# Moving the second layer's modulations from one feed-forward part beside another, and cutting that part in four groups

## Chip, cores and metric

The kernel runs on one core of one Trainium2 chip. The metric is the device time of one execution in microseconds, as the median of several executions. Times in the views of the profile come from one further execution, taken by the hardware profiler.

## What is computed

Two networks run one after the other on 512 tokens of width 1024, all in float32. The first is one layer of a hybrid block (16 meta tokens in front): a feed-forward part, a mix of forgetting attention and retention, and a second feed-forward part. The second network has two layers over 512 latent and (in the first layer) 256 context tokens. Cut to what matters here:

```
def swiglu(x, w_in, w_out):
    a, b = jnp.split(x @ w_in, 2, axis=-1)        # w_in 1024 x 2*2816
    return (jax.nn.silu(a) * b) @ w_out           # w_out 2816 x 1024

for l in range(2):
    mod   = split_cols(silu(c)     @ w_mod[l] + b_mod[l], (1024,) * 6)   # six vectors of 1024, for the latents
    mod_x = split_cols(silu(c_ctx) @ w_mod[l] + b_mod[l], (1024,) * 6)   # and six for the context
    h = layer_norm(x) * (1 + sc1) + sh1           # shift and scale come from mod
    ...                                           # mixing sublayer, gated by g1, layer norm
    x = layer_norm(ALPHA * x + g2 * swiglu_2(modulate(x, sh2, sc2), w_ffn_in[l], w_ffn_out[l])) ...
```

`w_mod[l]` is 1024 x 6144, so each layer's modulations read 25 MB and give only 12 vectors.

## The kernel before

**Layout.** Activations stand feature by feature: a tile is 128 features by a chunk of tokens. Each float32 operand is split into a high and a low part in fp32r, and each product is three matmuls into the same PSUM bank: high x high, high x low, low x high (`mm3`, lines 1334 to 1336; they show in the profile as weight tile and moving tile, each h or l).

**Weights.** SyncE loads every weight tile (128 x 1024, 512 KB, or less for output weights) in one written order into a ring of four buffers `Wf`. ScalarE copies it to a high part (L2054) and VectorE subtracts to get the low part (L2758); both go into a slot, three slots "base" and three "top" in the parts of interest. How many entries of the order the two engines may convert ahead of the one in use is `look`, set by the steps `("ahead", n)`; `AHEAD` is 1. TensorE waits for the low part at the first chunk of a tile (`tile_item`).

**Feed-forward parts.** 22 pairs of 128 inner features. For pair j the items "fa" (gate half, 8 slices of 3 matmuls) and "fb" (value half) give the hidden slice j: ScalarE takes the silu out of PSUM (L2332), VectorE multiplies (L3114), ScalarE makes the high part (L2342), POOL the low part (L3685). After a group of pairs, eight items "fo" multiply the hidden slices of the group with the output weights, and VectorE adds each result to `H` (`residual`, L3126). The groups are 8, 7 and 7 pairs in "f1" and "f2" (both parts of the first network) and in "g0" (first latent layer), and 5, 5, 6, 6 in "g1". f1 has chunks of 256 and 272 tokens, f2 two of 256, g0 three of 256 (context first). In f2 the second chunk runs four tiles behind the first. In g0 a `Group` deals out the items: the chunk that is furthest behind and whose norm is done is next, at most five tiles apart. The last group's "fo" items of g0 go chunk by chunk, and load their weights anew for each chunk, 24 weights for 24 items.

**Modulations.** A step `("mod", l, m)` takes one raw tile of `w_mod` from the ring; VectorE multiplies it with the silu of each of the two conditioning vectors and sums (`modulation`, L2972 and L2974, both 128 x 1024). Before the first step "vectors" lets POOL load the two vectors, spread over all partitions, into `CR` (L3701), and "rows" lets ScalarE take their silu (L2193). The 48 steps of layer 0 lie beside f1, those of layer 1 beside f2. Layer 1's results are first used after g0.

**Order.** All engines run the same written sequence. The planner `woven` writes it with a clock of its own: each matmul item costs 0.345 us for each slice, and the steps of a norm's chain (`chain`: mean, centre, square, root, second, both) are put in where their due times fall; later items wait for a gate, such as "chunk 0 of the next norm is done". After g0's last group come the norm of each chunk (d0 joined with a1) and the next layer's projections (`projection_items`), whose first eight items need chunk 0 alone, three need chunk 1, then three chunk 2. `FILL` puts filling matmuls (L1322) at a few places: 13 in the last chunk's mean, 15 and 3 ahead of the last chunk's first projection.

Of the kernel before, what the change touches and what calls it, by code (L numbers as in the profile page):

```python
# [4 lines left out]
F32 = mybir.dt.float32  # L5
# [12 lines left out]
T1 = NMETA + TX  # L18
NFF = 22
CH = [(0, 8), (8, 7), (15, 7)]  # L20
CHS = {"f1": CH, "f2": CH, "g0": CH, "g1": [(0, 5), (5, 5), (10, 6), (16, 6)]}
PLAIN_PAIRS = 3
UNITS_AHEAD = 7
ALPHA = (2 * 2) ** 0.25
# [101 lines left out]
class Shared:  # L126
# [42 lines left out]
    def buffers(self):  # L169
# [36 lines left out]
        self.H2[0], p = at("H2h", [128, 8, TX], F32R, P1)  # L206
        self.H2[1], p = at("H2l", [128, 8, TX], F32R, p)
        self.TM2, p = at("TM2", [128, 2, 256], F32, p)
        CR2, CR2e = at("CR2", [128, 1024], F32, p)

        self.YT, p = at("YT", [128, 4, 1024], F32, P1)
        self.YB, P2 = at("YB", [128, 8, TX], F32, p)
# [45 lines left out]
        self.OT, _ = at("OT", [128, 6, 1024], F32, P0)  # L258
        self.O[0], p = at("OH", [128, 8, 768], F32R, P4)
        self.O[1], P5 = at("OL", [128, 8, 768], F32R, p)  # L260
        self.H3[0], p = at("H3h", [128, 8, 768], F32R, P4)
        self.H3[1], p = at("H3l", [128, 8, 768], F32R, p)
        self.X2[1], P6 = at("X2l", [128, 8, 768], F32R, P5)
        self.XC2, _ = at("XC2", [128, 8, 768], F32, P5)
        assert CR2e <= P5
        self.PA, p = at("PA", [128, 3, 272], F32, P6)
        self.TM3, pm = at("TM3", [128, 3, 264], F32, p)
        self.MS, pm = at("MS", [128, 2, 128], F32, pm)
        self.WM_at = pm
        self.WM, pm = at("WM", [128, 2, 8, 64], F32, pm)  # L270
        assert pm <= TOP
        CR3, p = at("CR3", [128, 1024], F32, p)
        self.JK, p = at("JK", [128, 1024], F32, p)
        assert p <= TOP
        self.CR = [(CR1[:, 0, :], CR1[:, 1, :]), (CR2[:, :], CR3[:, :])]
        self.weight_slots("top", 3, TOP)

        self.QC, p = at("QC", [128, 3, 768], F32, P4)
# [538 lines left out]
class Group:  # L817

    def __init__(self, tiles, chunks, lead, gate):
        self.tiles, self.chunks, self.lead, self.gate = tiles, chunks, lead, gate
        self.at = {c: 0 for c in chunks}

    def due(self, ready):
        low = min(self.at.values())
        for c in sorted(self.chunks, key=lambda c: (self.at[c], c)):
            i = self.at[c]
            if i < len(self.tiles) and i - low < self.lead and ready(self.gate(c)):
                self.at[c] += 1  # L830
                k, x, nk = self.tiles[i]
                return (*k, x, c), 0.345 * nk, None
        return None

    def done(self):
        return min(self.at.values()) == len(self.tiles)


def woven(items, chains):
# [96 lines left out]
def second_sequence(p):  # L936

    f, n3, a = p.ffns["f2"], p.norms["n3"], p.norms["a0"]
    items = [(("open", "mixed", [(p.mm, ("branch", 1, 7, 0))]), 0, None)]
    items += [(("wo", m, c), 2.8, None) for m, c in lagged(range(8), 2, 4)]  # L940
    ends = [last_of(items, "wo", c, None) for c in (0, 1)]
    items[8:8] = [(("ahead", 2), 0, None)]
    items += [(("close", "mixed"), 0, None), (("open", "top", [(p.mm, ("mixout", 7, 1))]), 0, None)]
    items.append((("vectors", 1), 0, None))
    tiles = ffn_items(f, 4, lambda c: c, mod_steps(1))
    items += tiles[:8] + [(("ahead", AHEAD), 0, None)] + tiles[8:]
    done = last_of(items, "fb", 1, f)
    ends += [last_of(items, "fo", c, f) for c in (0, 1)]
    items += [(("close", "top"), 0, None), (("open", "latent", [(p.mm, ("fo", "f2", 2, 7, 1))]), 0, None)]
    items += projection_items(0, lambda c: 2 + c)  # L950
    chains = [(chain([n3], c), ends[c], 1.9) for c in (0, 1)] + [(chain([a], 0), done, 0.0)]
    chains += [(chain([a], c + 1), ends[2 + c], (3.5, 13.0)[c]) for c in (0, 1)]
    return woven(items, chains)
# [39 lines left out]
def latent_sequence(p, l):  # L993

    f, b, c_, d = p.ffns[f"g{l}"], p.norms[f"b{l}"], p.norms[f"c{l}"], p.norms[f"d{l}"]
    nc = len(f.chunks)
    ci = 1 if l == 0 else 0
    order = [3, 4, 5, 6, 7, 0, 1, 2]
    items = [("open", "top", p.fence(f"att{l}"))] + [("of", l, ci, k) for k in (3, 4)] + [("groups", l)]
    items += [("of", l, ci, k) for k in (5, 6, 7)] + [("scales", l)]  # L1000
    items += [("early", l, m, 0) for m in (0, 1)] + [("of", l, ci, k) for k in order[5:]] + [("ahead", 3)]
    for m in range(8):
        items.append(("oo", l, m, 0))
        if l == 0:
            items.append(("of", l, 0, order[m]))
        if m in (2, 5):
            items.append(("moments", b, m == 5))
    items = [(x, 2.8 if x[0] == "oo" else 0.5, None) for x in items]
    items += [(("oo", l, m, c), 2.8, None) for c in range(1, nc) for m in range(8)]
    if l == 0:  # L1010
        items[-2:-2] = [(("moments", d, False), 0, None)]
        items.append((("moments", d, True), 0, None))
    tiles = []
    last = len(CHS[f.tag]) - 1
    for n, (j0, nj) in enumerate(CHS[f.tag]):
        for j in range(j0, j0 + nj):
            tiles += [(("fa", f), j, 8), (("fb", f), j, 8)]
        if n < last:
            tiles += [(("fo", f), (n, m), nj) for m in range(8)]
    if l == 0:  # L1020
        items.append(Group(tiles, range(nc), 5, lambda c: c))
    else:
        items += fast_items(f, tiles)
    items += [(("fo", f, (last, m), c), 0.345 * CHS[f.tag][last][1], None) for c in range(nc) for m in range(8)]
    items += [(("ahead", AHEAD), 0, None), (("close", "top"), 0, None)]
    chains = [(chain([b], c), ("oo", l, 7, c), 3.0 if c == 2 else 2.0) for c in range(nc)]
    ends = [("fo", f, (last, 7), c) for c in range(nc)]
    if l == 0:
        items.append((("open", "latent", [(p.mm, ("fo", "g0", 2, 7, 2))]), 0, None))
        items += projection_items(1, lambda c: 3 + c)  # L1030
        chains += [(chain([d], c), ends[c], 2.0) for c in range(nc)]
        return woven(items, chains)
    chains += [(chain([d], c), ends[c], 2.0) for c in range(nc)]
    chains.append(([(("combine", f, x), 0.0, 2.5) for x in range(6)], ("fa", f, 0, 1), 0.5))
    return woven(items, chains)
# [1711 lines left out]
class VectorE(Engine):  # L2747
# [214 lines left out]
    def modulation(self, l, m):  # L2962

        p, e = self.p, self.e
        u = self.get("wmod", (l, m), 1024, True)
        w = p.Wf[:, u % NW, :]
        e.wait_ge(*p.w_arrived(u))
        if m == 0:
            e.wait_ge(*p.act.of(("rows", l, 1)))
        if m or l:  # L2970
            e.wait_ge(*p.dve.of(("first", l, m - 1) if m else ("first", l - 1, 47)))
        e.scalar_tensor_tensor(p.JK[:, :], w, 1.0, p.CR[l][0], ALU.mult, ALU.mult, p.MOD[:, l, m, 0:1]).then_inc(  # L2972
            *p.dve.did(("first", l, m)))
        e.scalar_tensor_tensor(w, w, 1.0, p.CR[l][1], ALU.mult, ALU.mult, p.MOD[:, l, m, 1:2]).then_inc(  # L2974
            *p.dve.did(("w", u), ("sum", l, m)))
        self.finished(u)
        if m % 8 < 7:
            return
        x = p.MOD[:, l, m - 7:m + 1, :]
        b0 = VEC[f"bmod{l}"][0] + m - 7  # L2980
        b = p.V[:, b0:b0 + 8].unsqueeze(2).broadcast_to([128, 8, 2])
        e.wait_ge(*p.dve.of(("sum", l, m)))
        if m // 8 in (2, 5):
            e.tensor_tensor(x, x, b, ALU.add).then_inc(*p.dve.did(("biased", l, m)))
            e.wait_ge(*p.dve.of(("biased", l, m)))
            e.tensor_scalar(x, x, 1.0 / ALPHA, None, ALU.mult).then_inc(*p.dve.did(("mod", l, m)))
        else:
            e.scalar_tensor_tensor(x, x, 1.0 if m // 8 in (1, 4) else 0.0, b, ALU.add, ALU.add).then_inc(
                *p.dve.did(("mod", l, m)))
# [653 lines left out]
class PoolE(Engine):  # L3643
# [8 lines left out]
    def step(self, what, *a):  # L3652
        p, e = self.p, self.e
        if what == "fb":
            self.hidden_low(*a)
        elif what == "load_sums":
            self.load_sums(*a)
        elif what == "apply":
            self.lows(*a)
        elif what == "both":  # L3660
            N, i, g = a
            if g == 1:
                self.lows(N.then, i)
        elif what == "bar":
            self.bar(*a)
            if a[0] == "mix":
                self.fence("mix")
                e.dma_start(p.CS[:, :, :], p.A["rope1"]).then_inc(*p.load(("rope1",)).did("in"))
                e.wait_ge(*p.load(("rope1",)).of("in"))
            else:  # L3670
                self.latent_loads(int(a[0][1]))
        elif what == "vectors":
            e.wait_ge(*p.mm.of(("mixout", 7, 1)))
            self.vectors(*a)
        elif what == "rturn":
            self.ret_turn(*a)
        elif what == "tick":
            self.tick(*a)
# [479 lines left out]
```

## Time and profile before

| | us |
|---|---|
| median of 3 executions | 3278.16 |
| lowest, highest | 3277.17, 3283.82 |
| the profiled execution | 3296.36 |
| its span in the trace | 3294.5 |
| TensorE busy | 3177.3 (96%) |
| VectorE busy | 1801.6 (55%) |
| ScalarE busy | 1391.9 (42%) |
| mean granted TensorE clock | 0.993 of full |

Times in the rows below are from the start of the span. A busy TensorE can still be slowed, since the ends of matmuls are modelled; only the distance of their starts and the waits tell the rest.

### The profile page before, as it was taken

The page shows a single profiled execution, that of the slowest core. Times are in us where ns is not written, and L with a number is a line of the kernel's source. Part 1 is how long each engine was busy: PE and PEld are TensorE (multiplying, and loading weights), DVE is VectorE, ACT ScalarE, POOL GpSimd, SP SyncE. Part 2 cuts the span into 40 slices and gives each one's busy share as a digit, 9 for nine tenths or more (in the row PEclk, how much of TensorE's full clock was granted, in tenths as well). Part 3 has the DMA queues.
Part 4 walks back from the last instruction along what each step waited for, and adds up shares of the span by engine and source line. Part 5 has one row for each costly group of instructions (what it writes and reads, how often), then busy time and mean ns, then how long its engine had stood idle before and what let it go on. Part 6 is the DMA issues. An engine that isn't in the chain of part 4 may idle for free. (4 is left out here: it accounts for less than half of the span.)

```text
span 3294.5 us, 60366 instructions
## 1 busy us (share of the span) xinstructions
PE 3177.3 (96%) x24458; PEld 2954.1 (90%) x24458; DVE 1801.6 (55%) x3099; ACT 1391.9 (42%) x2533; POOL 481.9 (15%) x471
## 2 busy tenths in 40 slices
PE   7999999999999999999999999999999999989998
PEld 7999988797778899998889889999998889979997
DVE  4666643536644456666435774222226646777766
ACT  4222232336633332225447755212124647665545
POOL 1010110036500010110103301101010103211110
PEclk9999999999999999999999999999999999999999
DMA  4445422122222334443211341211213311426663
GB/s 150 178 162 178 154 71 78 58 75 61 57 74 93 106 129 169 173 177 128 68 37 27 118 127 48 65 59 58 71 59 121 100 64 33 139 71 166 161 154 106
DMA packets 107075, 339.68 MB, mean 103 GB/s; under 512 B 12145, under 2 KB 16497, under 8 KB 106673
## 3 DMA queue, kind: packets, MB, share of 16 engines
q1 hardware_dynamic: 97616, 311.65, 28.9%
q0 software_dynamic: 8752, 23.65, 3.3%
q8 instruction: 198, 3.24, 0.4%
q14 instruction: 77, 0.62, 0.1%
q10 hardware_dynamic: 432, 0.52, 0.0%
HBM read 324.38 MB, written 2.10 MB: 99 GB/s over the span
## 5 line engine op out<-in xcount | busy, mean ns | idle before, releaser
L2758 DVE TENSOR_TENSOR r_Wbasel<-r_Wf,r_Wbaseh 128x1024 fp32r<-128x1024 f32 (+3 forms) x286 | 358.7, 1255 | 509.5 <-ACT r_Wbaseh L2054 509.0
L2054 ACT ACTIVATE r_Wbaseh<-r_Wf 128x1024 fp32r<-128x1024 f32 (+3 forms) x286 | 291.2, 1022 | 419.1 <-PE PS L1336 316.2
L2758 DVE TENSOR_TENSOR r_Wtopl<-r_Wf,r_Wtoph 128x1024 fp32r<-128x1024 f32 (+3 forms) x147 | 174.0, 1185 | 207.5 <-ACT r_Wtoph L2054 207.0
L1334 PE MATMUL PS<-r_X2h,r_Wbaseh 128*128 128x256 f32 (+1 forms) x888 | 276.7, 312 | 5.5 <-POOL r_X2l L3717 2.5
L1335 PE MATMUL PS<-r_X2l,r_Wbaseh 128*128 128x256 f32 (+1 forms) x888 | 269.0, 303 | 0.0
L1336 PE MATMUL PS<-r_X2h,r_Wbasel 128*128 128x256 f32 (+1 forms) x888 | 269.0, 303 | 0.0
L2054 ACT ACTIVATE r_Wtoph<-r_Wf 128x1024 fp32r<-128x1024 f32 (+3 forms) x147 | 145.9, 1001 | 141.6 <-PE PS L1336 54.6
L1334 PE MATMUL PS<-r_X1h,r_Wbaseh 128*128 128x512 f32 (+2 forms) x480 | 180.7, 376 | 8.5 <-ACT r_K L2455 3.2
L1334 PEld LDWEIGHTS PS<-r_X2h,r_Wbaseh 128*128 128x128 f32 x888 | 166.8, 188 | 19.0 <-POOL r_X2l L3717 3.3
L1336 PEld LDWEIGHTS PS<-r_X2h,r_Wbasel 128*128 128x128 f32 x888 | 169.1, 190 | 8.0
L1335 PEld LDWEIGHTS PS<-r_X2l,r_Wbaseh 128*128 128x128 f32 x888 | 166.8, 188 | 10.2 <-issue 2.6
L2332 ACT ACTIVATE r_TM<-PS 128x256 f32<-128x256 f32 (+1 forms) x160 | 61.4, 385 | 253.4 <-PE PS L1336 249.9
L1335 PE MATMUL PS<-r_X1l,r_Wbaseh 128*128 128x512 f32 (+2 forms) x480 | 168.3, 351 | 0.0
L1336 PE MATMUL PS<-r_X1h,r_Wbasel 128*128 128x512 f32 (+2 forms) x480 | 168.0, 350 | 0.0
L3114 DVE TENSOR_TENSOR r_TM<-r_TM,PS 128x256 f32<-128x256 f32 (+1 forms) x160 | 67.1, 420 | 148.7 <-PE PS L1336 136.5
L1334 PE MATMUL PS<-r_X2h,r_Wtoph 128*128 128x256 f32 x504 | 141.7, 281 | 0.0
L1335 PE MATMUL PS<-r_X2l,r_Wtoph 128*128 128x256 f32 x504 | 141.5, 281 | 0.0
L1336 PE MATMUL PS<-r_X2h,r_Wtopl 128*128 128x256 f32 x504 | 141.5, 281 | 0.0
L2974 DVE SCALAR_TENSOR_TENSOR r_Wf<-r_Wf,r_CR 128x1024 f32<-128x1024 f32 x96 | 131.1, 1366 | 0.0
L3378 DVE TENSOR_REDUCE r_SM<-PS 128x1 f32<-128x768 f32 (+6 forms) x184 | 120.9, 657 | 18.2 <-PE PS L1878 12.5
L3126 DVE SCALAR_TENSOR_TENSOR r_H<-PS,r_MOD,r_H 128x256 f32<-128x256 f32 x136 | 65.4, 482 | 118.4 <-PE PS L1336 117.8
L2972 DVE SCALAR_TENSOR_TENSOR r_JK<-r_Wf,r_CR 128x1024 f32<-128x1024 f32 x96 | 117.5, 1224 | 0.0
(544 smaller groups left out, 11105.8 us busy)
## 6 DMA issues: line engine op xcount, KB each, us to landing
r_Wf<-in_wmod SPq DMA_DIRECT2D x96, 512.0 KB, 3.6
r_Wf<-in_f_in SPq DMA_DIRECT2D x88, 512.0 KB, 4.4
r_Wf<-in_g_in SPq DMA_DIRECT2D x69, 512.0 KB, 3.5
r_Wf<-in_w_o SPq DMA_DIRECT2D x40, 512.0 KB, 4.4
r_Wf<-in_f_out SPq DMA_DIRECT2D x32, 448.0 KB, 4.2
r_Wf<-in_g_out SPq DMA_DIRECT2D x32, 448.0 KB, 3.4
r_SR<-in_g_in SPq DMA_DIRECT2D x38, 256.0 KB, 3.7
r_SR<-in_g_in POOLq DMA_DIRECT2D x38, 256.0 KB, 5.4
```

Of the source, the lines that this page charges most:

```text
L1334: self.e.matmul(o, wh, xh, start=first, stop=False)
L1335: self.e.matmul(o, wh, xl, start=False, stop=False)
L1336: return self.e.matmul(o, wl, xh, start=False, stop=last)
L2054: e.activation(p.w(i, cols)[0], p.Wf[:, i % NW, 0:cols], ACT.Copy).then_inc(*p.hi.did(i))
L2332: e.activation(f.tm(j, c), p.psb(p.bank(("fa", f.tag, j, c)), f.chunks[c][1]), ACT.Silu).then_inc(*p.act.did(("silu", f.tag, j, c)))
L2758: e.tensor_tensor(l, p.Wf[:, i % NW, 0:cols], h.bitcast(F32), ALU.subtract).then_inc(*p.lo.did(i))
L2972: e.scalar_tensor_tensor(p.JK[:, :], w, 1.0, p.CR[l][0], ALU.mult, ALU.mult, p.MOD[:, l, m, 0:1]).then_inc(*p.dve.did(("first", l, m)))
L2974: e.scalar_tensor_tensor(w, w, 1.0, p.CR[l][1], ALU.mult, ALU.mult, p.MOD[:, l, m, 1:2]).then_inc(*p.dve.did(("w", u), ("sum", l, m)))
L3114: e.tensor_tensor(x, x, p.psb(p.bank(("fb", f.tag, j, c)), f.chunks[c][1]), ALU.mult).then_inc(*p.dve.did(("gated", f.tag, j, c)))
L3126: e.scalar_tensor_tensor(hk, p.psb(p.bank(("fo", f.tag, ci, m, c)), n), f.gate(m, c0), hk, ALU.mult, ALU.add).then_inc(*p.dve.did(("res", ...
L3378: e.tensor_reduce(p.SM[:, u % 4:u % 4 + 1], p.psb2(b, 0, d.n), AX, ALU.max, negate=True).then_inc(*p.dve.did(("max", A.id, u)))
```

## The change

The 48 modulation steps of layer 1, with "vectors" and "rows", leave f2 and are handed to g0's `Group` as `others`: after 12 tile items, one of the 51 entries is dealt out after every 180/51 = 3.5 tile items (of 204 in the group; the last group's 24 "fo" items come after it). The first of the entries is `("ahead", AHEAD)`, so `look` goes from 3 to 1 there. g0's groups become 6, 6, 5, 5 pairs, so that `H3` needs six slices; in the space of the other two lie the conditioning vectors `CR2` and a scratch tile `JK2` of layer 1. "vectors" now waits for the last output projection before g0.

```diff
-CHS = {"f1": CH, "f2": CH, "g0": CH, "g1": [(0, 5), (5, 5), (10, 6), (16, 6)]}
+CHS = {"f1": CH, "f2": CH, "g0": [(0, 6), (6, 6), (12, 5), (17, 5)], "g1": [(0, 5), (5, 5), (10, 6), (16, 6)]}
...
-        CR2, CR2e = at("CR2", [128, 1024], F32, p)
...
-        self.H3[0], p = at("H3h", [128, 8, 768], F32R, P4)
-        self.H3[1], p = at("H3l", [128, 8, 768], F32R, p)
+        self.H3[0], p = at("H3h", [128, 6, 768], F32R, P4)
+        self.H3[1], p = at("H3l", [128, 6, 768], F32R, p)
+        CR2, p = at("CR2", [128, 2, 1024], F32, p)
+        JK2, p = at("JK2", [128, 1024], F32, p)
+        assert p <= P5
...
-        CR3, p = at("CR3", [128, 1024], F32, p)
-        self.JK, p = at("JK", [128, 1024], F32, p)
+        JK1, p = at("JK1", [128, 1024], F32, p)
         assert p <= TOP
-        self.CR = [(CR1[:, 0, :], CR1[:, 1, :]), (CR2[:, :], CR3[:, :])]
+        self.CR, self.JK = [(t[:, 0, :], t[:, 1, :]) for t in (CR1, CR2)], (JK1, JK2)
...
-    def __init__(self, tiles, chunks, lead, gate):
+    def __init__(self, tiles, chunks, lead, gate, others=()):
         self.tiles, self.chunks, self.lead, self.gate = tiles, chunks, lead, gate
-        self.at = {c: 0 for c in chunks}
+        self.at, self.others, self.said = {c: 0 for c in chunks}, others, 0

     def due(self, ready):
-        low = min(self.at.values())
+        low, n = min(self.at.values()), len(self.others)
+        if self.said < n and self.said * (len(self.at) * len(self.tiles) - 24) < (sum(self.at.values()) - 12) * n:
+            self.said += 1
+            return self.others[self.said - 1], 0, None
...
-    items.append((("vectors", 1), 0, None))
-    tiles = ffn_items(f, 4, lambda c: c, mod_steps(1))
+    tiles = ffn_items(f, 4, lambda c: c)
...
-        items.append(Group(tiles, range(nc), 5, lambda c: c))
+        items.append(Group(tiles, range(nc), 5, lambda c: c, [("ahead", AHEAD), ("vectors", 1)] + mod_steps(1)))
...
-        items.append((("open", "latent", [(p.mm, ("fo", "g0", 2, 7, 2))]), 0, None))
+        items.append((("open", "latent", [(p.mm, ("fo", "g0", 3, 7, 2)), (p.dve, ("sum", 1, 47))]), 0, None))
...
-            e.wait_ge(*p.mm.of(("mixout", 7, 1)))
+            e.wait_ge(*p.mm.of(("oo", 0, 7, 2)))
```

## Rows read from the trace of the kernel before

**Rows 1.** The page: busy engines, and the commonest conversion groups.

```profile
span 3294.5 us, 60366 instructions
PE 3177.3 (96%) x24458; PEld 2954.1 (90%) x24458; DVE 1801.6 (55%) x3099; ACT 1391.9 (42%) x2533; POOL 481.9 (15%) x471
...
L2758 DVE TENSOR_TENSOR r_Wbasel<-r_Wf,r_Wbaseh 128x1024 fp32r<-128x1024 f32 (+3 forms) x286 | 358.7, 1255 | 509.5 <-ACT r_Wbaseh L2054 509.0
L2054 ACT ACTIVATE r_Wbaseh<-r_Wf 128x1024 fp32r<-128x1024 f32 (+3 forms) x286 | 291.2, 1022 | 419.1 <-PE PS L1336 316.2
```

**Rows 2.** Windows: length; PE, PEld, DVE, ACT, POOL; clock, DMA share, GB/s.

```profile
1163.00:1535.00 372.00, 363.41 (x3132) 356.47 (x3133) 240.44 (x367) 115.77 (x176) 42.81 (x45) 1.00 0.45 156
2018.00:2504.00 486.00, 486.00 (x4128) 485.93 (x4126) 128.69 (x185) 111.33 (x187) 45.88 (x62) 1.00 0.22 69
```

**Rows 3.** Waits of TensorE, 1163 to 1533: us in total, times, longest.

```profile
PE PS L1334 <- DVE r_Wbasel L2758: 3.1, 6, 0.7
PE PS L1334 <- DVE r_Wtopl L2758: 3.1, 5, 1.1
```

**Rows 4.** Windows of 10 us; the first count is of matmuls.

```profile
1240.00:1250.00 10.00, 10.00 (x90) 10.00 (x89) 8.03 (x13) 2.78 (x4) 1.21 (x1) 1.00 0.50 167
1290.00:1300.00 10.00, 10.00 (x87) 10.00 (x86) 6.94 (x11) 2.92 (x4) 0.73 (x1) 1.00 0.49 177
2260.00:2270.00 10.00, 10.00 (x87) 10.00 (x87) 2.09 (x4) 2.17 (x4) 1.48 (x2) 1.00 0.14 46
```

**Rows 5.** Timeline of TensorE: starts of matmuls.

```profile
2557.01 0.28 PE L1334 MATMUL PS<-r_H3h,r_Wtoph 128*128 128x256 f32 x1
...
2557.69 0.28 PE L1334 MATMUL PS<-r_X2h,r_Wbaseh 128*128 128x256 f32 x1
...
2010.96 0.39 PE L1334 MATMUL PS<-r_X2h,r_Wbaseh 128*128 128x256 f32 x1 [1.24 <-POOL r_X2l L3717]
...
2011.42 0.28 PE L1334 MATMUL PS<-r_X2h,r_Wbaseh 128*128 128x256 f32 x1
...
2012.48 0.28 PE L1334 MATMUL PS<-r_X2h,r_Wbaseh 128*128 128x256 f32 x1
```

**Rows 6.** VectorE groups: 1163 to 1533 (two), 2018 to 2503.

```profile
L2974 DVE SCALAR_TENSOR_TENSOR r_Wf<-r_Wf,r_CR 128x1024 f32<-128x1024 f32 x48 | 65.5, 1364 | 0.0
L2972 DVE SCALAR_TENSOR_TENSOR r_JK<-r_Wf,r_CR 128x1024 f32<-128x1024 f32 x48 | 59.1, 1231 | 0.0
L3126 DVE SCALAR_TENSOR_TENSOR r_H<-PS,r_MOD,r_H 128x256 f32<-128x256 f32 x56 | 27.1, 484 | 90.2 <-PE PS L1336 90.2
```

**Rows 7.** DMA issues over the span: KB each, median us to landing.

```profile
r_Wf<-in_wmod SPq DMA_DIRECT2D x96, 512.0 KB, 3.6
r_CR<-in_c POOLq DMA_DIRECT2D x4, 512.0 KB, 5.3
```

**Rows 8.** Timeline of VectorE and POOL at g0's end.

```profile
2508.20 2.35 DVE L3007 TENSOR_TENSOR r_H<-r_H,PS 128x1024 f32<-128x1024 f32 x2
2519.83 0.43 DVE L3047 TENSOR_SCALAR r_RS<-PS 128x256 f32<-128x256 f32 x1 [1.74 <-ACT r_RS L2267]
...
2524.65 0.41 DVE L3063 TENSOR_TENSOR r_SQ<-PS,r_RS 128x256 f32<-128x256 f32 x1
...
2553.73 2.41 POOL L3717 TENSOR_TENSOR r_X2l<-r_XC,r_X2h 128x1024 fp32r<-128x1024 f32 x1 [70.06 <-ACT r_X2h L2306]
...
2613.63 2.36 POOL L3717 TENSOR_TENSOR r_X2l<-r_XC,r_X2h 128x1024 fp32r<-128x1024 f32 x1 [19.59 <-ACT r_X2h L2306]
```

**Rows 9.** Waits of TensorE, 2503 to 2620.

```profile
PE PS L1625 <- ACT r_SQ L2251: 4.4, 2, 2.3
```

**Rows 10.** A window and two starts of TensorE in the last layer.

```profile
2930.00:2940.00 10.00, 6.88 (x40) 6.60 (x41) 5.10 (x4) 6.17 (x10) 3.10 (x2) 0.83 0.05 10
...
2935.20 0.41 PE L1334 MATMUL PS<-r_X3h,r_Wtoph 128*128 128x256 f32 x1
2935.42 0.41 PE L1335 MATMUL PS<-r_X3la,r_Wtoph 128*128 128x256 f32 x1
```

More of the change, by code:

```diff
@@ L260, in buffers @@
         self.O[1], P5 = at("OL", [128, 8, 768], F32R, p)
-        self.H3[0], p = at("H3h", [128, 8, 768], F32R, P4)
-        self.H3[1], p = at("H3l", [128, 8, 768], F32R, p)
+        self.H3[0], p = at("H3h", [128, 6, 768], F32R, P4)
[3 more added lines that the diff above has]
+        assert p <= P5
         self.X2[1], P6 = at("X2l", [128, 8, 768], F32R, P5)
         self.XC2, _ = at("XC2", [128, 8, 768], F32, P5)
-        assert CR2e <= P5
         self.PA, p = at("PA", [128, 3, 272], F32, P6)
@@ L835, in done @@
     def done(self):
-        return min(self.at.values()) == len(self.tiles)
+        return min(self.at.values()) == len(self.tiles) and self.said == len(self.others)
 def woven(items, chains):
@@ L2971, in modulation @@
             e.wait_ge(*p.dve.of(("first", l, m - 1) if m else ("first", l - 1, 47)))
-        e.scalar_tensor_tensor(p.JK[:, :], w, 1.0, p.CR[l][0], ALU.mult, ALU.mult, p.MOD[:, l, m, 0:1]).then_inc(
+        e.scalar_tensor_tensor(p.JK[l][:, :], w, 1.0, p.CR[l][0], ALU.mult, ALU.mult, p.MOD[:, l, m, 0:1]).then_inc(
             *p.dve.did(("first", l, m)))
```

## The prediction

> **What bounds the kernel now.** I read the page first. TensorE is busy 96% of the span, VectorE 55%, so work taken off VectorE is worth nothing by itself; only what it makes TensorE wait for counts [rows 1]. Then the windows, stage by stage [rows 2]. In the first net's second feed-forward part ("f2", 1163 to 1535 us) VectorE is at 240/372 = 65% and the DMA engines move 156 GB/s. In the steady part of the first latent layer's feed-forward part ("g0", 2018 to 2504) TensorE is busy all 486 us, VectorE 26%, DMA 69 GB/s. So the 48 modulation steps leave a full stage for an empty one, but TensorE is nearly full in both: the whole prize is the waits in f2 and what happens at g0's two ends.
>
> The waits say how much there is: in f2 TensorE waited 3.1 + 3.1 = 6.2 us, eleven times, for a weight's low half (L2758), which VectorE had not finished [rows 3]. In g0's steady part the view of waits is empty (no idle time in rows 2 either).
>
> A second thing shows only in windows of 10 us. Without idle time TensorE starts 90 matmuls of 256 columns in some and 87 in others [rows 4]. Between starts there are 113.3 ns in the fast pace (2557.01 to 2557.69 is six) and 117.8 ns in the slow one (2010.96 aside, 2011.42 to 2012.48 is nine) [rows 5]; the granted clock is 1.00, its level of 2.4 GHz, in both. Going through the starts, the pace changes only where TensorE restarts after a gap, and then holds. In f2 it is slow from 1262 to 1307, from 1395 to 1440 and for some 10 us later, 100 us in all; in g0 it is slow from the restart at 2010.96 until 2504 without a break. Slow costs 4.5/117.8 = 3.8%.
>
> **The change, part by part.**
>
> *Modulations out of f2.* 48 pairs of VectorE instructions of 1.23 and 1.36 us, 125 us, leave [rows 6], with 48 loads of 512 KB [rows 7]. VectorE falls to 115/372 = 31%, near g0's 26%, where TensorE never waits, and the ring of four load buffers serves weights alone. I take all 6.2 us. Without restarts the pace in which f2's body begins should hold; it is fast there before the first step's work (the last restart at 1165 was a fast one), so the 100 us of slow pace go too: 3.8 us. Bounds of that: if f2 ran slow throughout, 264 us more would be slow (1170 to 1534 less the 100), each 113.3 growing by 4.5: +10.4 us; if the share of slow pace stays, 0.
>
> The Trainium skill ("TensorE: Matmul & The Clock Gate", section "Back-to-back issue gap") gives one gap for warm matmuls, N/2.4 + 2.5 ns, which is 109 ns at 256 columns. The rows differ from it and have two paces; by that rule no pace term would exist and the sum would hold the 6.2 us alone.
>
> *Modulations into g0.* The 51 added entries (a lookahead setting, "vectors", "rows", 48 steps) are spread over 204 - 24 tile items, one in 3.5 items, which is 3.5 x 24 x 0.118 = 10 us; each costs VectorE 2.6 us. VectorE: 129 + 125 + 12 (below) = 266 of 486 us, 55%. DMA: 25 MB more over 486 us, 69 + 52 = 121 GB/s against the 156 that f2 lived with [rows 2]. More telling than shares is the lead. In f2 a weight serves two chunks, and the second runs four tiles behind, so five of six slots are held and a new weight has 5.4 us. In g0 three chunks go in step, a weight serves 3 items of 2.8 us = 8.5 us; in the output groups 6.4 us (six slices) and 5.3 us (five). The work that can stand before the low half is one step 2.6, a gating or residual 0.48 and the conversions 1.0 + 1.25 [rows 1]: 5.3 us. It fits, with nothing to spare at five slices. The new lookahead of 1 (g0 ran at 3) still lets the next weight through across one step. I take 0; the bounds are 0 and f2's rate of 0.13 us a step, 6.2 us. SyncE's queue holds a step's load between two weights: 3.6 us to landing [rows 7], four ring slots are some 18 us ahead. POOL issues two loads of 512 KB (5.3 us to landing) four items, 11 us, before ScalarE needs them; if they were late ScalarE would stand still, but eight PSUM banks hold 22 us of TensorE's work. The scratch tiles lie in slices 6 and 7 of H3, which six-slice groups don't touch, and the O tiles there are dead by then.
>
> *Four groups.* The matmuls are the same: 22 slices x 8 x 3 chunks x 3. VectorE gets 24 more residual adds of 0.484 us, 11.6 us [rows 6], hidden under TensorE. The third boundary needs the last pair's hidden half; two boundaries of the same kind cost nothing today, and a step of 2.6 us before them still ends within the 7.4 us that the item order leaves. 0, at worst 1 us.
>
> *g0's end.* Here I expect a loss. The last group goes chunk by chunk, 24 items with a weight each. They shrink from 21 matmuls (2.4 us) to 15 (1.75 us), and run now at lookahead 1 instead of 3: a weight is converted two items ahead, 3.5 us, not four, 9.8 us. Yet the norm chain of a finished chunk puts blocks on VectorE: the root 2519.83 to 2525.06, 5.2 us; the centring 2.35; the second root and its products [rows 8]. Today three conversions run ahead of the root and TensorE loses nothing to weights there (its largest waits, 4.4 us in all, are for the chain itself) [rows 9].
>
> Stepping the queues from the end of chunk 0 (today 2501.7), with these durations: waits for weights of about 1.7 us after the centring, 2.3 after the first root, 2.1 and 2.2 around the second root's products; all 16 items of the other chunks end after 46 us (today 2557.7 - 2501.7 = 56). But the written order, made with 1.725 us an item, now has chunk 1's root ahead of chunk 0's last products, so chunk 0's inputs for the next projections are done after about 60 us (root at 42.7 + 1.6, ScalarE free at 48, root 5.2 to 54, products 2.5 and 3.1, high and low halves) against 54.4 today (POOL's low half 2553.73 + 2.41) [rows 8]. From there the projections need 44.6 us until the last chunk's second half (8 + 3 items of 2.75, the chain's 3.5, 18 filling matmuls 7.9, half an item). The total work is the same and 16 x 6 = 96 matmuls fewer lie behind chunk 0, so it ends 96 x 0.116 = 11.1 us later than today. New mark: 2501.7 + 11.1 + 60 + 44.6 = 2617.4; today 2616.0 [rows 8]. +1.3 us. Bounds: chunk 0 ready at 53 (the chain unimpeded), -5.7; at 68, +9.3.
>
> **Sum.** -6.2 - 3.8 + 0 + 0 + 1.3 = -8.7 us. The profiled execution took 3296.4 us (span 3294.5 and 1.9 around it), 18.2 above the median of 3278.2; the sum is a difference and I set it against the median: 3269.5 us. That 18.2 us are also what a fast g0 would be worth warns me that timed runs may sit in other paces.
>
> **Rivals.**
> - *g0 flips to the fast pace.* One restart in g0, from a step that makes a weight late, or another phase at its start. 486 x 3.8% = 18.6 us for all of it. For it: most restarts in f2 went fast. Against: few waits are expected there. 3269.5 - 18.6 = 3251; half of it 3260.
> - *f2 settles in the slow pace.* Nothing restarts it any more. -6.2 + 1.3 + 6.7 (170 us more slow than today) to + 10.4: 3280 to 3284. Against: its last restart before the steps was a fast one, and that part of the order stays.
> - *No pace effect.* The share of slow pace stays what it is, in f2 and in g0: -6.2 + 1.3, 3273. For it: whatever picks the pace is not known, and f1, whose chunks are 256 and 272 wide, is slow nearly throughout. The single gap on the Trainium skill's page ("TensorE: Matmul & The Clock Gate") would give this too.
> - *The steps are late in g0* (slower). VectorE's 2.6 us before a low half, at lookahead 1, in the output groups of 5.3 us a tile. It decides from 0.2 us a step: 48 x 0.2 = 9.6 eats the gain; at 0.5, +24, 3294. For it: f2 did so at 4.8 us a tile (42 matmuls). Against: the lead above.
> - *The end costs more.* Chunk 0 ready after 68 us: +9.3. An idle stretch there can also lower the clock: after 3.79 us idle at 2933 the granted clock reads 0.83 over 10 us and starts are 210 to 220 ns apart, the 1.2 GHz level, for 4 us, 2 us lost [rows 10]. 3278 to 3280.
>
> **Chances.** Forecast 0.40 (own range 3262 to 3276); fast g0 0.20; slow f2 0.12; no pace effect 0.13; late steps 0.10; dear end 0.05. Range 3251 to 3284, which leaves out the better half of fast g0 and most of late steps. What a measurement of this kernel can tell from no change is about 0.2%, 6.6 us. Faster by more: 0.27 + 0.18 + 0.06 + 0.02 = 0.53. Slower by more: 0.10 + 0.03 + 0.02 = 0.15. Within: 0.32.
>
> **What would show it.** Right: no wait of an L1334 on L2758 in f2, and 90 matmuls in its 10 us windows; g0's steady part still without waits; in the last group new waits on L2758 of 1 to 2 us, and an idle stretch of TensorE before the first projection. Wrong: waits on L2758 through g0's body, or 90 in its windows instead of 87; f2's windows at 87; a last group without waits for weights.

## The result, and the profile after

The kernel after takes 3298.20 us (median of 4, 3296.84 to 3299.51), the kernel before 3278.59 on the same chip: ratio 1.0056, 95% interval 1.0044 to 1.0069. It is slower by 0.56%, 18 to 20 us. I had forecast 3269.5.

In the kernel after, the lines I follow stand two further down: L1334 to L1336 are L1336 to L1338, L2758 is L2760, L2239 is L2241. First the same windows as [rows 2], then one over the tail of g0 and one of 10 us in it.

```profile
1163.00:1535.00 372.00, 369.85 (x3262) 365.42 (x3262) 135.99 (x178) 122.55 (x191) 37.27 (x46) 1.00 0.30 94
2018.00:2504.00 486.00, 484.51 (x4287) 481.57 (x4286) 262.24 (x432) 121.16 (x207) 47.35 (x58) 1.00 0.36 121
2480.00:2620.00 140.00, 100.35 (x761) 89.77 (x760) 83.50 (x112) 69.88 (x118) 9.27 (x7) 0.88 0.30 95
2590.00:2600.00 10.00, 5.49 (x25) 5.50 (x26) 8.08 (x9) 5.78 (x6) 2.35 (x1) 0.50 0.38 121
```

In the 372 us of f2 TensorE now starts 3262 matmuls and not 3132: 130 more, at 113.3 ns 14.7 us. VectorE is at 136/372 = 37% there, and its 262 us in g0 cost TensorE nothing before the last group. The loss is in the third row: 40 us of 140 idle. Before, the same 140 us had TensorE busy for 130.31:

```profile
2480.00:2620.00 140.00, 130.31 (x1066) 118.76 (x1066) 98.69 (x128) 80.46 (x128) 10.61 (x9) 0.98 0.35 110
```

The waits of TensorE from 2455 to 2640 in the kernel after: total, times, longest.

```profile
PE PS L1336 <- DVE r_Wbasel L2760: 17.0, 4, 12.1
PE PS L1695 <- ACT r_PA L2241: 8.2, 1, 8.2
PE PS L1649 <- ACT r_PA L2241: 6.8, 1, 6.8
PE PS L1627 <- DVE r_H L3128: 4.7, 1, 4.7
PE PS L1336 <- DVE r_Wtopl L2760: 3.0, 2, 1.5
PE PS L1978 <- ACT r_SQA L2644: 0.3, 1, 0.3
```

40.0 us, where the first profile of before has 10.0 in this stretch. Four waits are long (12.1, 8.2, 6.8, 4.7), and all four begin after the last output item of g0 has ended (2524.8).

What stood in front of the weight for which TensorE waited 12.06 us shows in ScalarE's timeline, with TensorE's restart behind it:

```profile
2575.74 1.04 ACT L2056 ACTIVATE r_Wbaseh<-r_Wf 128x1024 fp32r<-128x1024 f32 x1
...
2576.95 2.06 ACT L2294 ACTIVATE r_H<-r_H,r_V 128x256 f32<-128x256 f32 x4
...
2580.82 2.08 ACT L2294 ACTIVATE r_H<-r_H,r_V 128x256 f32<-128x256 f32 x4 [0.96 <-DVE r_H L3069]
2584.72 2.08 ACT L2305 ACTIVATE r_XC<-r_XC,r_MOD 128x256 f32<-128x256 f32 x4 [1.82 <-DVE r_XC L3088]
2586.83 1.06 ACT L2308 ACTIVATE r_X2h<-r_XC 128x1024 fp32r<-128x1024 f32 x1
2587.79 2.06 ACT L2305 ACTIVATE r_XC<-r_XC,r_MOD 128x256 f32<-128x256 f32 x4
2589.88 1.06 ACT L2308 ACTIVATE r_X2h<-r_XC 128x1024 fp32r<-128x1024 f32 x1
2590.84 1.04 ACT L2056 ACTIVATE r_Wbaseh<-r_Wf 128x1024 fp32r<-128x1024 f32 x1
```
```profile
2594.51 0.58 PE L1336 MATMUL PS<-r_X2h,r_Wbaseh 128*128 128x256 f32 x1 [12.06 <-DVE r_Wbasel L2760]
2594.89 0.41 PE L1337 MATMUL PS<-r_X2l,r_Wbaseh 128*128 128x256 f32 x1
2595.10 0.41 PE L1338 MATMUL PS<-r_X2h,r_Wbasel 128*128 128x256 f32 x1
```

Between two conversions of weights (2575.74 and 2590.84) stand the second root, its products and both halves of chunk 2's last step. Chunk 2 is needed by TensorE last of all; the conversion behind its blocks is needed now. When TensorE restarts, its starts are 0.21 us apart: over the idle stretch the granted clock fell to the level of 1.2 GHz (0.50 in the window of 2590). Some 29 matmuls start at that distance, and they take about 3 us more than at the fast pace.

The cause is to be read in the written order. Items of TensorE are in brackets, a number behind "d0" is a chunk; both lists begin behind the last output item of g0.

```
before: second d0 1 [qk 6] mean d0 2 [qk 8] both d0 1 0, centre d0 2 [qk 9] [vc 0] square d0 2, both d0 1 1
        [vc 1] root d0 2 [vc 2] second d0 2, both d0 2 0, both d0 2 1 [vc 3] [qk 2, chunk 0] ...
after:  mean d0 2, centre d0 2, second d0 1 [qk 6] both d0 1 0, square d0 2 [qk 8] root d0 2,
        both d0 1 1 [qk 9] second d0 2, both d0 2 0, both d0 2 1 [vc 0] [vc 1] [vc 2] [vc 3] [qk 2, chunk 0] ...
```

Before, chunk 2's chain is spread over five items, from behind [qk 6] to ahead of [vc 3]; after, all of it stands ahead of [vc 0], over three items. TensorE reaches [vc 3] with weights that were converted ahead of the bunch's end; the wait of 12.06 us is for the weight of the item behind it, [qk 2, chunk 0]. The planner's clock ran with items of five slices; on it the chains of chunks 1 and 2 fell due while it waited for chunk 0, and it wrote them down there.

The other half of the surprise is the kernel before itself. Its first profiled execution took 3296.4 us, 18 more than its timed ones. So the first run is that kernel once more.

### The profile page after: what moved, and what is told of

It reads as the page before. It is cut to its first block and busy times, and to the rows that moved or that the text cites. A ratio compares the mean times of both kernels' runs of the same rounds, so it can differ in the third digit from the quotient of the medians.

```text
span 3295.0 us, 60461 instructions
## 1 busy us (share of the span) xinstructions
PE 3151.4 (96%) x24458; PEld 2933.8 (89%) x24458; DVE 1809.8 (55%) x3131; ACT 1388.7 (42%) x2541; POOL 480.1 (15%) x471
## 5 line engine op out<-in xcount | busy, mean ns | idle before, releaser
L2760 DVE TENSOR_TENSOR r_Wbasel<-r_Wf,r_Wbaseh 128x1024 fp32r<-128x1024 f32 (+3 forms) x291 | 359.4, 1237 | 565.6 <-ACT r_Wbaseh L2056 565.2
L1336 PE MATMUL PS<-r_X2h,r_Wbaseh 128*128 128x256 f32 (+1 forms) x864 | 271.0, 314 | 17.8 <-DVE r_Wbasel L2760 15.6
L2760 DVE TENSOR_TENSOR r_Wtopl<-r_Wf,r_Wtoph 128x1024 fp32r<-128x1024 f32 (+3 forms) x150 | 171.8, 1146 | 171.6 <-ACT r_Wtoph L2056 171.6
L1337 PE MATMUL PS<-r_X2l,r_Wbaseh 128*128 128x256 f32 (+1 forms) x864 | 262.3, 304 | 0.0
L1338 PE MATMUL PS<-r_X2h,r_Wbasel 128*128 128x256 f32 (+1 forms) x864 | 262.2, 303 | 0.0
L1336 PEld LDWEIGHTS PS<-r_X2h,r_Wbaseh 128*128 128x128 f32 x864 | 164.9, 191 | 31.1 <-DVE r_Wbasel L2760 17.2
L1336 PE MATMUL PS<-r_X1h,r_Wbaseh 128*128 128x512 f32 (+2 forms) x480 | 180.7, 377 | 8.6 <-ACT r_K L2457 3.2
L1337 PEld LDWEIGHTS PS<-r_X2l,r_Wbaseh 128*128 128x128 f32 x864 | 165.0, 191 | 10.4 <-issue 2.6
L1338 PEld LDWEIGHTS PS<-r_X2h,r_Wbasel 128*128 128x128 f32 x864 | 164.8, 191 | 8.0
L1338 PE MATMUL PS<-r_X1h,r_Wbasel 128*128 128x512 f32 (+2 forms) x480 | 168.0, 350 | 0.0
L1336 PE MATMUL PS<-r_X2h,r_Wtoph 128*128 128x256 f32 x528 | 146.0, 277 | 0.0
L1338 PE MATMUL PS<-r_X2h,r_Wtopl 128*128 128x256 f32 x528 | 145.8, 276 | 0.0
L3380 DVE TENSOR_REDUCE r_SM<-PS 128x1 f32<-128x768 f32 (+6 forms) x184 | 121.0, 657 | 17.1 <-PE PS L1880 11.0
L3687 POOL TENSOR_TENSOR r_H3l<-r_TM,r_H3h 128x256 fp32r<-128x256 f32 x66 | 54.8, 832 | 445.8 <-ACT r_H3h L2344 445.8
```

The costliest lines, as they stand in the source:

```text
L1336: self.e.matmul(o, wh, xh, start=first, stop=False)
L1337: self.e.matmul(o, wh, xl, start=False, stop=False)
L1338: return self.e.matmul(o, wl, xh, start=False, stop=last)
L2760: e.tensor_tensor(l, p.Wf[:, i % NW, 0:cols], h.bitcast(F32), ALU.subtract).then_inc(*p.lo.did(i))
L3380: e.tensor_reduce(p.SM[:, u % 4:u % 4 + 1], p.psb2(b, 0, d.n), AX, ALU.max, negate=True).then_inc(*p.dve.did(("max", A.id, u)))
```

## Experiments

Each was timed against the kernel before on the same chip, with as many runs as stand beside it (the first with one). Where two traces are compared I use the time between two marks in g0: the restart on chunk 2's second half at its start, and the same of the last chunk's first projection at its end.

**1. The kernel before once more.** No edit.

> The kernel before, once more with a profile, to see which of two things its first profiled execution of 3296.4 us (18 over its timed runs) was. Theory A (the pace of g0 differs from execution to execution, and the first profile caught a slow one): if this profile is near 3278, g0's windows of 10 us show 90 matmuls and not 87 and the stretch 2010 to 2504 is up to 18 us shorter. Rival B (profiling adds the 18 us everywhere): 3296 again, windows as before.

3280.78 us, and its windows:

```profile
2018.00:2504.00 486.00, 486.00 (x4298) 483.97 (x4297) 139.88 (x201) 121.96 (x202) 45.74 (x62) 1.00 0.23 74
2260.00:2270.00 10.00, 10.00 (x91) 10.00 (x90) 1.51 (x2) 3.26 (x6) 0.73 (x1) 1.00 0.16 48
```
```profile
2011.41 0.39 PE L1334 MATMUL PS<-r_X2h,r_Wbaseh 128*128 128x256 f32 x1 [1.28 <-POOL r_X2l L3717]
...
2598.03 0.38 PE L1334 MATMUL PS<-r_X2h,r_Wbaseh 128*128 128x256 f32 x1 [1.31 <-POOL r_X2l L3717]
```

4298 matmuls in the stretch where [rows 2] has 4128, 91 in the window where [rows 4] has 87. Between the marks (2598.03 - 2011.41) lie 586.6 us; in the first profile it is 2616.04 - 2010.96 = 605.1; the start is in [rows 5], and the end mark reads

```profile
2616.04 0.38 PE L1334 MATMUL PS<-r_X2h,r_Wbaseh 128*128 128x256 f32 x1 [1.29 <-POOL r_X2l L3717]
```

Theory A holds: the same program ran g0 in the slow pace once and in the fast pace here, and the difference of 18.5 us is that of the executions (3296.4 to 3280.8, 15.6) with 3 us elsewhere the other way. The timed median goes with the fast one. All twelve profiles of this section and that of the kernel after show g0 fast; the first one of before was the odd one of fourteen. The baseline for the marks is 586.6; in the kernel after they are at 1995.69 and 2617.67, 622.0 apart: 35.4 us lost, of which 40.0 - 10.1 = 29.9 are waits.

Where they are lost shows when the stretch is cut at two more starts: the first output item of chunk 1 (chunk 0's last one has then ended) and the first projection item. For the kernel after, with the end mark:

```profile
2478.60 0.28 PE L1336 MATMUL PS<-r_H3h,r_Wtoph 128*128 128x256 f32 x1
...
2544.44 0.78 PE L1336 MATMUL PS<-r_X2h,r_Wbaseh 128*128 128x256 f32 x1
...
2617.67 0.47 PE L1336 MATMUL PS<-r_X2h,r_Wbaseh 128*128 128x256 f32 x1
```

| us | start mark to end of chunk 0's output items | to the first projection | to the end mark |
|---|---|---|---|
| before, first profile | 490.5 | 56.2 | 58.4 |
| before, this run | 472.0 | 57.3 | 57.3 |
| after | 482.9 | 65.8 | 73.2 |

The first column grows by 10.9 us, because 96 more matmuls now lie ahead of that point. The other two grow by 8.5 and 15.9 us.

**2. The four groups alone.**

```diff
-CHS = {"f1": CH, "f2": CH, "g0": CH, ...
+CHS = {"f1": CH, "f2": CH, "g0": [(0, 6), (6, 6), (12, 5), (17, 5)], ...
```

> The kernel before with g0's groups 6, 6, 5, 5 alone: modulations stay in f2, lookahead stays 3, memory as before. Theory O (the order written for shorter last items puts all of chunk 2's norm chain ahead of the fourth projection item, and TensorE runs out of work twice): slower than before by 15 to 25 us, 3293 to 3304, with waits of TensorE of about 30 us between 2480 and 2620 and one of 10 us or more before the item vc 0. Rival L (it is the lookahead of 1 that the moved steps bring): within 3 us of before, 3276 to 3282.

3312.29 us (4 runs; before 3281.58), ratio 1.0096 (1.0082 to 1.0110): +30.7. Its waits in the tail:

```profile
PE PS L1334 <- DVE r_Wbasel L2758: 13.8, 2, 12.1
PE PS L1693 <- ACT r_PA L2239: 11.2, 2, 7.6
PE PS L1647 <- ACT r_PA L2239: 7.2, 1, 7.2
PE PS L1625 <- DVE r_H L3126: 3.3, 1, 3.3
```

The whole loss, and more, is in the groups, with the modulations still in f2 and the lookahead at 3. Theory O had the size of the waits (35.8 us with a small one of 0.3, the longest 12.1), but not the place of the longest, which stands ahead of [qk 2, chunk 0] and not of vc 0; and the time is 8 us above its range.

**3. The lookahead of 3 in the last group.** On the kernel after:

```diff
+    if l == 0:
+        items.append((("ahead", 3), 0, None))
     items += [(("fo", f, (last, m), c), 0.345 * CHS[f.tag][last][1], None) for c in range(nc) for m in range(8)]
```

> The kernel after, with the lookahead put back to 3 ahead of the last group's output items; its written order stays. Theory O (the order): the waits of 1.4 to 1.9 us for weights in the last group go, at most 6 us, but the long ones at 2525 to 2594 stay, since they lie where the lookahead is 3 in both kernels: 3292 to 3298. Rival L (the lookahead): most of the 30 us of waits go, 3268 to 3275.

3298.30 us (5 runs; before 3281.58), ratio 1.0054 (1.0041 to 1.0067): +16.7, where the kernel after has +19.6, and 0.3 above theory O's range. Between the marks are 616.6 us, 5.4 less than in the kernel after. The small waits of the last group are gone, and the others, 34.2 us, are those of run 2 but for one (10.4 where that has 12.1):

```profile
PE PS L1338 <- DVE r_Wbasel L2762: 12.2, 2, 10.4
PE PS L1697 <- ACT r_PA L2243: 11.2, 2, 7.6
PE PS L1651 <- ACT r_PA L2243: 7.2, 1, 7.2
```

The long waits stand where they stood, behind the last output item, where the lookahead is 3 in both kernels. The lookahead isn't the cause of the large part.

**4. The old order, on the kernel after.** The planner prices the last group's items at seven slices; items and instructions stay. The written tail is then that of before.

```diff
-    items += [(("fo", f, (last, m), c), 0.345 * CHS[f.tag][last][1], None) for ...
+    items += [(("fo", f, (last, m), c), 0.345 * (7 if l == 0 else CHS[f.tag][last][1]), None) for ...
```

> The kernel after, with the planner's price for the last group's output items put back to that of seven slices, which writes the tail in the same order as in the kernel before (chunk 2's steps spread between the projection items); nothing else changes. Theory O (the order): 3265 to 3278, 20 to 30 us faster than after, the wait of 12.06 us gone. Rival S (the items are simply too short to cover the chains, whatever the order): within 5 us of after, 3293 to 3299. Rival L (the lookahead of 1): the same as rival S.

3281.23 us (11 runs, 3270.62 to 3300.31; before 3281.58), ratio 1.0004 (0.9988 to 1.0019): 17 us less than the kernel after, 20.0 by what each has against its own runs of before, and 3 us above theory O's range. The runs spread over 30 us, so the second figure is not exact to more than a few us. The wait of 12 us is gone; what is left are three of about 3 us for weights in the last group:

```profile
PE PS L1336 <- DVE r_Wbasel L2760: 5.9, 2, 3.2
PE PS L1336 <- DVE r_Wtopl L2760: 3.1, 1, 3.1
```

**5. The new order, on the kernel before.** The opposite edit: groups of 8, 7, 7 with their seven-slice items, priced at five. Nothing else differs from the kernel before.

> The kernel before (8, 7, 7 pairs, modulations in f2, lookahead 3) with one thing changed: the planner prices the last group's output items at five slices, so that the tail of g0 is written in the order of the kernel after, while the items keep their seven slices. Theory O (the written order is what costs): slower than before by 15 to 30 us, 3297 to 3312, with waits of TensorE near 30 us in the tail and one of about 12 us for a weight ahead of vc 0. Rival S (short items leave the chains uncovered, the order alone is harmless): within 5 us of before, 3277 to 3287.

3302.57 us (5 runs; before 3279.12), ratio 1.0078 (1.0066 to 1.0090): +23.5.

```profile
PE PS L1334 <- DVE r_Wbasel L2758: 13.5, 2, 12.0
PE PS L1693 <- ACT r_PA L2239: 8.2, 2, 7.3
PE PS L1625 <- DVE r_H L3126: 6.0, 1, 6.0
PE PS L1647 <- ACT r_PA L2239: 4.9, 1, 4.9
```

The four long waits come with the order alone, long items or short. Of the 26.2 us between the marks (612.8 for 586.6), 12.9 lie ahead of the first projection and 13.3 behind it.

**6. Only chunk 2's chain later.** On the kernel after; the order of chunks 0 and 1 in the last group stays new.

```diff
-        chains += [(chain([d], c), ends[c], 2.0) for c in range(nc)]
+        chains += [(chain([d], c), ends[c], 12.0 if c == 2 else 2.0) for c in range(nc)]
```

> The kernel after, with only chunk 2's norm chain due 10 us later in the planner: its six entries then stand between the projection items again, while the order of the chains of chunks 0 and 1 in the last group stays that of after. Theory O2 (the loss is chunk 2's bunch in front of vc 0 alone): 3275 to 3283. Theory O1 (the late order of chunk 0's and 1's steps costs its share, the waits of 4.7, 6.8 and 8.2 us): 3285 to 3293. Rival S: 3294 to 3299.

3278.97 us (11 runs, 3272.74 to 3280.83; before 3279.12), ratio 0.9998 (0.9989 to 1.0007). Between the marks 601.1 us, 20.9 less than in the kernel after. By the times it takes away as much as the whole old order did in run 4 (which still has 9.0 us of waits for weights in the last group). Of the 20.9 us, 16.0 lie behind the first projection, which needs 57.2 us to the end mark, as in the kernel before: that part was chunk 2's bunch. Ahead of the first projection 61.0 us are left of 65.8, and there stands one long wait. It is for chunk 0's inputs: it ends with the first projection item, which needs chunk 0 alone, before chunk 2's chain has begun.

```profile
2538.14 0.55 PE L1336 MATMUL PS<-r_X2h,r_Wbaseh 128*128 128x256 f32 x1 [14.65 <-DVE r_X2l L3092]
```
```profile
PE PS L1336 <- DVE r_X2l L3092: 14.7, 1, 14.7
PE PS L1336 <- DVE r_Wbasel L2760: 3.5, 2, 1.9
PE PS L1336 <- DVE r_Wtopl L2760: 3.0, 2, 1.5
```

**7. The old order and the lookahead of 3.** The edits of 3 and 4 together.

> The kernel after with the old tail order and the lookahead of 3 in the last group, both. Theory: with the old order the lookahead matters (it left waits of 3.15, 3.17 and 2.74 us for weights and a stretch at 1.2 GHz behind them, 12 us in all against the second profile of before), so this takes 8 to 12 us off the run with the old order alone: 3269 to 3273. Rival (the order leaves no room for the lookahead, as it changed nothing with the new order): 3279 to 3283.

3268.88 us (7 runs, 3266.34 to 3276.12; before 3279.12), ratio 0.9975 (0.9965 to 0.9986): -10.2 against before, where run 4 has -0.35. With the old order the lookahead counts for 9.9 us (6.0 between the marks).

```profile
PE PS L1629 <- ACT r_SQ L2255: 4.4, 2, 2.3
PE PS L1651 <- ACT r_PA L2243: 4.0, 2, 2.2
PE PS L1629 <- DVE r_H L3130: 1.9, 1, 1.9
PE PS L1629 <- DVE r_H L3011: 1.6, 1, 1.6
PE PS L1338 <- DVE r_Wbasel L2762: 1.4, 1, 1.4
PE PS L1338 <- POOL r_X2l L3721: 1.3, 1, 1.3
```

The waits are 14.9 us with the small one. The marks are 2587.03 - 1995.33 = 591.7 us apart, 5.1 more than before. The first projection starts at 2528.24, 50.0 us behind chunk 0's output items, and from there 58.8 us pass to the end mark.

**8. A longer last group: 5, 5, 6, 6.** On run 7:

```diff
-"g0": [(0, 6), (6, 6), (12, 5), (17, 5)]
+"g0": [(0, 5), (5, 5), (10, 6), (16, 6)]
```

> As the run with both, but with g0's groups 5, 5, 6, 6 instead of 6, 6, 5, 5, so that the last group's 24 items have 18 matmuls each, not 15. Theory S (a part of the tail's cost is that short items cover less of the chains): 2 to 6 us below the run with both. Rival (the tail is bound by the chains' own length from the last output item on, which grows by nothing): within 1.5 us of it.

3272.90 us (12 runs, 3265.31 to 3282.37; before 3279.12), ratio 0.9981 (0.9971 to 0.9991). It is 4 us above run 7, where theory S had it 2 to 6 below and its rival within 1.5; the two intervals overlap, and between the marks it has 589.9 us, 1.8 less, so which is better stays open. The waits in its tail are 2.2 us less in all (12.7 for 14.9).

**9. A lookahead of 5 for the projections.** On the kernel after, in its own order:

```diff
-    items = [(("ahead", 3), 0, None)] + [(("qk", l, s, True, True, 0), 2.8, gate(0)) for s in (6, 8, 9)]
+    items = [(("ahead", 5 if l else 3), 0, None)] + ...
```

> The kernel after, in its own written order, with the lookahead in the second layer's projections at 5 instead of 3. Theory Q (the wait of 12.06 us is a conversion queued behind chunk 2's blocks on ScalarE and VectorE: lookahead 3 reaches from the step before the bunch to vc 3 and no further, the next weight stands behind): two more weights pass ahead of the bunch, the wait shrinks to about half and 5 to 10 us come back, 3288 to 3293. Rival (that weight is late for another reason, its load or its slot): 3296 to 3300.

3299.00 us (6 runs, 3293.77 to 3303.54; before 3282.17), ratio 1.0050 (1.0038 to 1.0063). The profile goes with theory Q: TensorE takes nine items, not seven, before the wait, which is now for the weight of the tenth.

```profile
2599.87 0.58 PE L1336 MATMUL PS<-r_X2h,r_Wlatenth 128*128 128x256 f32 x1 [8.00 <-DVE r_Wlatentl L2760]
```

It gives back 4.1 of the 12.1 us there, but the conversions moved ahead of the blocks delay the chain, whose waits grow from 8.2 and 6.8 us to 9.0 and 7.8. Between the marks are 617.3 us, 4.6 less than in the kernel after, where 5 to 10 were expected. The time is in the rival's range and not in theory Q's: +16.8 us over before, against +19.6, with intervals that overlap. That the wait moved to the weight two entries further on shows that it is the queue behind the bunch, as theory Q has it, and not that weight's load or slot; a longer reach is hardly a remedy while the bunch stays.

**10. Chunk 2's chain later and the lookahead of 3.** Runs 6 and 3 together.

> The run with chunk 2's chain written later, and the lookahead of 3 in the last group as well. The waits for weights of the last group (3.0 and 3.5 us in the run without it) go: 3 to 7 us below it, 3272 to 3276. Rival (TensorE then waits as much longer for chunk 2's inputs, where it already waits 14.7 us): no change, 3277 to 3281.

3277.57 us (12 runs, 3271.06 to 3283.55; before 3282.17), ratio 0.9988 (0.9978 to 0.9998). The waits for weights are gone, and the one ahead of the first projection grew from 14.7 to 17.1 us; like that of run 6 it is for chunk 0's inputs, not for chunk 2's as the rival says. The median is 1.4 us below run 6 and lies in the rival's range; by what each has against its own runs of before it is 4.5 us, which is theory's 3 to 7. They are not told apart.

Runs 3, 10 and 7 differ in the order alone, at five slices and lookahead 3: +16.7, -4.6 and -10.2 us. Chunk 2's chain is worth 21.3 us of the 27.0. The other 5.6 (6.6 between the marks) belong to the order of chunks 0 and 1 in the last group: there the first projection waits until 59.9 us behind chunk 0's output items, and 50.0 with the old order.

**11. The modulations without VectorE's time.** On the kernel before; each of the two vector instructions of a layer 1 step works on 64 columns, so layer 1's modulations are left out for the most part.

```diff
+        k = 64 if l else 1024
-        e.scalar_tensor_tensor(p.JK[:, :], w, 1.0, p.CR[l][0], ...
+        e.scalar_tensor_tensor(p.JK[:, 0:k], w[:, 0:k], 1.0, p.CR[l][0][:, 0:k], ...
```

> The kernel before with the 96 vector instructions of the second layer's modulations cut to 64 of their 1024 columns (this leaves out most of each sum, so the second layer is computed with wrong modulations); their loads, their places in the order and the ring stay. Theory V (what the modulations cost in f2 is VectorE's time ahead of a low half): the eleven waits of f2 go and 12 to 15 us with them, 3264 to 3268. Rival D (it is the loads and the ring of four buffers, which the change takes away too): less than 4 us, 3275 to 3280.

3264.50 us (5 runs; before 3282.17), ratio 0.9945 (0.9933 to 0.9957): -17.7. TensorE's waits from 1163 to 1533 are then:

```profile
PE PS L1625 <- DVE r_H L3127: 1.5, 1, 1.5
PE PS L1334 <- POOL r_X5l L3718: 0.7, 1, 0.7
PE PS L1334 <- DVE r_X5l L3107: 0.3, 1, 0.3
```

All 48 loads are still there; what f2 paid was VectorE's time. From the restart on chunk 2's second half in g0 to the end mark nothing changed (586.6 us).

**12. The four groups in the old order.** On run 2, the edit of run 4.

> The kernel before with g0's groups 6, 6, 5, 5, and the tail written in the old order (planner's price of seven slices for the last group's output items); modulations stay in f2, lookahead 3. It fills the square of order and item size. Theory O (the order is nearly all of the loss, the shorter items cost by themselves about what was forecast for g0's end, 1.3 us, at most 9): within 4 us of before, 3278 to 3286. Rival S (short items cost ten or more by themselves, and the order only the rest): 3290 to 3296.

3286.57 us (11 runs, 3279.84 to 3290.94; before 3280.55), ratio 1.0019 (1.0009 to 1.0030): +6.0, just outside theory O's range (within 4 us, at most 3286) and far below rival S's. With it the square is full, each against its own runs of before, modulations in f2 and lookahead 3:

| | seven slices (8, 7, 7) | five slices (6, 6, 5, 5) |
|---|---|---|
| old order | 0 | +6.0 |
| new order | +23.5 | +30.7 |

Between the marks the same four have 586.6 and 591.7 us in the upper row, 612.8 and 616.2 in the lower. The order costs 23.5 and 24.7 us by the times (26.2 and 24.5 by the marks), the short items 6.0 and 7.2 (5.1 and 3.4). To move the modulations gives 14.0 us in the new order (run 2 to run 3) and 16.3 in the old (run 12 to run 7).

## Why the prediction was wrong

*The step that failed* is "from there the projections need 44.6 us until the last chunk's second half". They needed 2617.67 - 2544.44 = 73.2. The result lies 19.6 + 8.7 = 28.3 us from the forecast, and this step alone is off by 28.6; what else missed nearly cancels (chunk 0 ready 5.8 us later than forecast, the start mark 15.7 us earlier than before where 10.0 were forecast). The 28.6 us are two errors.

The first has nothing to do with the change. In the kernel before the same interval is 58.4 us in the first profile (2557.69 in [rows 5] to 2616.04, which I had as 2616.0) and 57.3 in the second. The terms that I gave for 44.6 add up to 43, and "the chain's 3.5" was mis-sized: what TensorE does and waits for between the items for chunk 2's mean, centre, square and root takes 13.9 us in run 1 (2543.53 to 2550.48 alone is the mean with its 13 filling matmuls). The new mark was built up from this sum and then set against the measured one of today, and so 44.6 - 58.4 = -13.8 us went into the forecast as a gain that nothing stood for. With 58.4 the sum would have been +15.1 at g0's end, and 3283 us.

The second is the written order. I knew that it had changed, and followed the change only to chunk 0's last products; behind them stands the larger one, chunk 2's chain in front of the weights. It costs 15.9 us in this interval (73.2 for 57.3), and run 6 gives back 16.0 of it by moving that chain alone. By itself the order costs 23.5 us (run 5), about half of it ahead of the first projection.

The rival "the end costs more" had the right place and sign, but its upper bound held the same 44.6; only chunk 0's readiness was varied (+9.3), so no case reached +20.

*g0's end up to that point* was right in its parts. The waits for weights in the last group were forecast at 1.7, 2.3, 2.1 and 2.2 us; four came, of 1.49, 1.88, 1.49 and 1.63. The 16 items of chunks 1 and 2 were to end after 46 us and ended after 46.2 (2478.60 to 2524.84). Chunk 0 was to be ready after 60 us; its first item started after 65.8, within the upper bound of 68.

*Modulations out of f2*: right, and worth more than 10.0 us. No wait for a weight is left, and the pace is fast from 1165.5 to 1482. By times it is 14.0, 16.3 or 17.7 us (the square, run 11). Part of the shortfall is how I priced a wait. Around the largest of the eleven:

```profile
1394.06 0.28 PE L1336 MATMUL PS<-r_H2h,r_Wtopl 128*128 128x256 f32 x1
1395.48 0.39 PE L1334 MATMUL PS<-r_X5h,r_Wtoph 128*128 128x256 f32 x1 [1.14 <-DVE r_Wtopl L2758]
1395.70 0.28 PE L1335 MATMUL PS<-r_X5l,r_Wtoph 128*128 128x256 f32 x1
```

The view says 1.14 us idle, but the starts are 1.42 apart where 0.113 is usual, and the next 0.22: 1.42 + 0.22 - 0.23 = 1.41. Over the eleven this makes 9.2 us where the view of waits lists 6.2. With 3.8 for the pace that is 13.0; from the restart at 1165 to the first projection item behind f2 the kernel after takes 14.4 us less than the first profile of before (368.7 to 354.3) and 13.4 less than the second.

*Modulations into g0*: right, 0. The view of waits is empty from 2012 to 2480 in run 7, at 262 of 486 us of VectorE in the kernel after. The rival of late steps is out.

*Four groups*: 0 for g0's body holds (the view of waits is empty from 2012 to 2470 in run 12, with the modulations in f2), but the groups set the planner's price of the last items, and so the order. I had put them down as the same matmuls and 24 more adds.

*A fast g0* came true and was worth nothing: the second profile of before is fast there already, and the timed runs of before lie with it. To set the difference against the median was right, but a fast g0 could then not also be a case below it. No pace effect and a slow f2 did not happen.

With the old order and lookahead 3 (run 7) the time is 3268.9 us, against 3269.5 forecast, but this is luck. Chunk 0 is ready 50.0 us behind its output items and not 60, the projections need 58.8 and not 44.6; the marks lie 5.1 us further apart than before where the sum had +1.3, and f2 gave 16.3 us where the sum had 10.0. This version beats the kernel before by 0.25%, just above what can be told from no change.

## What to carry over

When a change alters a number from which a planner writes the order, write down both orders to the end of the stretch, and compare entry by entry what stands in front of each weight conversion. Check every sum of the kind "from here TensorE is the bound" against the same interval in the kernel before; if that doesn't come out, the bound is another. A term that is built up on one side of a difference must be built up on the other side too. And where one profiled execution is 18 us off the timed ones, take it again before a single pace or wait is priced from it.

## What the runs showed of the hardware

- The same program ran some 490 us of g0 at 117.8 ns between starts in one execution and at 113.3 in another, at a granted clock of 1.00 in both: 18.5 us between the marks. Thirteen of fourteen profiles were fast there. In both executions the pace was set at the restart near 2011 and held.
- A wait costs TensorE 0.27 us more than its idle time in the view (9.2 us for 6.2 in eleven waits; 9.6 for 6.4 in twelve in the second profile).
- In the kernel after TensorE's starts were 0.21 us apart, the level of 1.2 GHz, behind its waits of 6.79 and 12.06 us; behind those of 1.49 to 1.88 us they were not.
- Where a low half that VectorE makes of a weight (L2760, 128x1024) overlaps POOL's making of an activation's low half, it takes 2.53 to 2.57 us in the kernel after (2542.48, 2576.81, 2591.92), and 1.2 otherwise. The last of the three is in the wait of 12.06 us: some 1.3 us of it are this.
